# A two-block model's last stage: expert weights in 2 MB pieces and nine slots, one expert gathered ahead, output summed and normed as rows

## The reference

```python
h2 = modulate(rmsnorm(x, norm2_g[l]), sh2, sc2)
x = x + g2 * ec_moe(h2, router_w[l], exp_w1[l], exp_w3[l], exp_w2[l])
return rmsnorm(x, final_g)

def ec_moe(h, router_w, w1, w3, w2):
    aff = jax.nn.softmax(jnp.einsum('bnd,de->bne', h, router_w), axis=-1)
    gates, idx = lax.top_k(jnp.swapaxes(aff, 1, 2), cap)
    xg = jax.vmap(lambda hb, ib: hb[ib])(h, idx)
    a = jnp.einsum('becd,edf->becf', xg, w1)
    b = jnp.einsum('becd,edf->becf', xg, w3)
    y = jnp.einsum('becf,efd->becd', jax.nn.silu(a) * b, w2)
    y = y * gates[..., None]
    return scatter_add(y, idx)
```

## Time and profile before

| | |
|---|---|
| Median of 3 runs | 2808.36 us (2807.79 to 2813.71) |
| The profiled execution | 2808.7 us |
| its span, first to last instruction | 2806.9 us |
| TensorE busy | 2324.2 us, 83% |
| VectorE, ScalarE busy | 776.9 and 345.4 us |
| DMA | 709.05 MB (here of a million bytes), mean 253 GB/s |
| mean granted TensorE clock | 0.883 of 2.4 GHz |

### The profile page before, as it was taken

One profiled execution on the slowest core, in us unless ns is written; L12 is line 12 of the kernel. 1 busy time (PEld: TensorE's weight loads), 2 busy tenths in 40 slices (PEclk: granted clock), 3 DMA queues, 4 the chain that ended last, 5 costly groups with the idle time before them and its releaser, 6 DMA issues.

```text
span 2806.9 us, 34475 instructions
## 1 busy us (share of the span) xinstructions
PE 2324.2 (83%) x14480; PEld 1578.5 (56%) x14480; DVE 776.9 (28%) x1449; ACT 345.4 (12%) x600; POOL 8.7 (0%) x13
## 2 busy tenths in 40 slices
PE   6999879999999899899999986896666666666665
PEld 5887668888888689888877766751011111111111
DVE  5555434474001464411043229340000000000001
ACT  1102221101011222111012110210000000000001
POOL 0000000000000100000000000000000000000000
PEclk9999989999999899999999998887777777677677
DMA  8888234886344230144333120479999999999996
GB/s 339 361 343 357 90 135 190 361 343 237 141 164 164 105 135 4 48 159 156 136 120 120 60 75 1 162 308 418 418 416 416 418 418 418 418 417 416 418 418 279
DMA packets 114085, 709.05 MB, mean 253 GB/s; under 512 B 10833, under 2 KB 10961, under 8 KB 44497
## 3 DMA queue, kind: packets, MB, share of 16 engines
q1 hardware_dynamic: 114000, 707.80, 63.1%
HBM read 706.71 MB, written 1.05 MB: 252 GB/s over the span
## 4 chain that ended last, share of the span: by engine, by line
PE 62%; DMA 25%; DVE 7%; SPq 4%; ACT 1%; issue 1%; DVEq 0%; ACTq 0%
DMA ring<-in_w 17%; PE ps L656 11%; PE ps L670 11%; PE ps L663 11%; DMA sq<-in_w 6%; PE ps L699 5%; PE ps L1009 4%; PE ps L815 4%; SPq L558 3%; PE ps L1189 2%; PE ps L629 1%; PE ps L1227 1%; PE ps L1007 1%; PE ps L1216 1%; PE ps L728 1%
## 5 line engine op out<-in xcount | busy, mean ns | idle before, releaser
L656 PE MATMUL ps<-hT,arena 128*128 128x256 f32 x1408 | 325.6, 385 | 10.0 <-ACT hT L1303 10.0
L663 PE MATMUL ps<-hT,arena 128*128 128x256 f32 x1408 | 318.2, 379 | 0.0
L670 PE MATMUL ps<-hid,arena 128*128 128x256 f32 x1408 | 311.1, 379 | 0.0
L656 PEld LDWEIGHTS ps<-hT,arena 128*128 128x128 f32 x1408 | 271.9, 194 | 53.2 <-issue 15.2
L663 PEld LDWEIGHTS ps<-hT,arena 128*128 128x128 f32 x1408 | 267.5, 190 | 36.4
L670 PEld LDWEIGHTS ps<-hid,arena 128*128 128x128 f32 x1408 | 267.5, 190 | 36.4
L1189 PE MATMUL ps<-ring,arena 128*32 128x512 f32 x1024 | 172.4, 770 | 79.7 <-DMA ring<-in_w 78.1
L1275 ACT ACTIVATE arena<-ps 128x512 f32<-128x512 f32 (+5 forms) x152 | 95.9, 641 | 1014.6 <-PE ps L1206 316.2
L1189 PE MATMUL ps<-arena 128*32 128x512 f32 x768 | 146.6, 855 | 81.7 <-DMA arena<-in_w 81.7
L1216 PE MATMUL ps<-arena 128*32 128x512 f32 x768 | 132.2, 793 | 78.1 <-DMA arena<-in_w 65.9
L1664 DVE TENSOR_TENSOR hid<-sil,ps 128x256 f32<-128x256 f32 x88 | 37.1, 421 | 577.1 <-ACT sil L1313 576.8
(11 more groups left out here) (347 smaller groups left out, 2117.8 us busy)
## 6 DMA issues: line engine op xcount, KB each, us to landing
arena<-in_w SPq DMA_DIRECT2D x192, 1024.0 KB, 24.0
ring<-in_w SPq DMA_DIRECT2D x128, 1024.0 KB, 20.7
arena<-in_ada SPq DMA_DIRECT2D x96, 1024.0 KB, 10.4
ring<-in_ring_w SPq DMA_DIRECT2D x52, 1024.0 KB, 4.9
arena<-in_ffn_gate SPq DMA_DIRECT2D x44, 1024.0 KB, 5.7
arena<-in_ffn_up SPq DMA_DIRECT2D x44, 1024.0 KB, 6.4
arena<-in_ffn_down SPq DMA_DIRECT2D x44, 1024.0 KB, 4.8
hT<-in_w SPq DMA_DIRECT2D x32, 1024.0 KB, 18.1
```

The costliest lines, as they stand in the source:

```text
L656: last = mm(ps[:, ft, 0:T], gate3[:, kt, ft * P:(ft + 1) * P], h3[:, kt, :], start=kt == 0, stop=kt == KT - 1)
L663: last = mm(ps[:, ft, T:2 * T], up3[:, kt, ft * P:(ft + 1) * P], h3[:, kt, :], start=kt == 0, stop=kt == KT - 1)
L670: last = mm(acc(m), down3[:, ft, m * P:(m + 1) * P], hid3[:, ft, :], start=False, stop=True, skip_group_check=True)
```

## The change

- The host lays the weights out anew, as one array `experts` of pieces of 2 MB, 12 for each expert: four of w1, four of w3, four of w2, each with one contiguous row of 16 KB for each partition.
- There are nine slots of 2 MB: six places of `arena`, two halves of `ring`, and `hT` and `sq` together (now one tensor `hT_sq`). SyncE issues two loads and `earlier` after `hy_mixed`, four loads after `hg_out`, two as the projection frees the ring, one after the third `e_turned`, and each later one when the piece nine back is used.
- The logits come first, with the router as the weights (eight matmuls of 256 columns) and are then transposed; the transposes of `h` follow them. Spreading needs 16 rooms in other banks. VectorE ranks expert 0 alone, then experts 1 to 15.
- `picked(e)` makes one expert's tokens and its way back: 16 matmuls of 32 columns, two transposes. It is called for expert e + 1 between the second and the third piece of w2 of expert e. The big gather and `way_back` are gone.
- The output is summed as rows (tokens on the partitions) in four banks; `x` is put there by 16 matmuls during expert 0, the gate is applied to `e_y` by VectorE, and the last norm works along the rows: a square with a sum, a root and a reciprocal of one column, two products and a store of half the output for each 128 tokens.
- The experts are straight code on all engines in place of hardware loops.

The core of the diff (blank lines taken out):

```diff
+    w13 = np.stack([np.asarray(i["exp_w1_2"])[0], np.asarray(i["exp_w3_2"])[0]], 1)
+    w13 = w13.reshape(NE, 8, 2, P, EFF).transpose(0, 1, 3, 2, 4).reshape(NE, 8, P, 2 * EFF)
+    w2 = np.asarray(i["exp_w2_2"])[0].reshape(NE, 4, 4, P, D).transpose(0, 1, 3, 2, 4).reshape(NE, 4, P, 4 * D)
+    out["experts"] = np.concatenate([w13, w2], 1).reshape(NE * PER_EXPERT, P, 2 * SLOT)
...
+        hT_sq = sb("hT_sq", 2 * KT * T)
+        hT, sq = hT_sq[:, 0:KT * T], hT_sq[:, KT * T:]
...
+        e_slots = [ar(n, 2 * SLOT) for n in (0, 2 * SLOT, 13056, 19200, 19200 + 2 * SLOT, 19200 + 4 * SLOT)] \
+            + [ring[:, 0:2 * SLOT], ring[:, 2 * SLOT:], hT_sq[:, :]]
+        E_RING = len(e_slots)
...
+            def expert_load(n):
+                if n >= E_RING:
+                    sp.wait_ge(sem("moe_slot"), n - E_RING + 1)
+                sp.dma_start(e_slots[n % E_RING], a["experts"][n, :, :]).then_inc(sem(E_LANDED[n % E_RING][0]), 16)
...
+            sp.wait_ge(sem("hy_mixed"), 4)
             sp.dma_start(e_early.rearrange("p a b -> p (a b)"), a["earlier"]).then_inc(sem("early_landed"), 16)
...
-            with sp.Fori(0, NE - 1) as e:
-                for j in range(E_RING, PER_EXPERT):
-                    sp.wait_ge(sem("moe_slot"), PER_EXPERT * e + (j - E_RING + 1))
-                    expert_load(e, j)
...
+            for n in range(2):
+                expert_load(n)
+            sp.wait_ge(sem("hg_out"), 1)
+            for n in range(2, 6):
+                expert_load(n)
+            for n in range(6, 8):
+                sp.wait_ge(sem("proj_slot"), 8 + 2 * (n - 6) + 2)
+                expert_load(n)
+            sp.wait_ge(sem("e_turned"), 3)
+            for n in range(8, PER_EXPERT * NE):
+                expert_load(n)
+            for tt in range(TT):
+                sp.wait_ge(sem("row_ready"), tt + 1)
+                sp.dma_start(out[tt * P:(tt + 1) * P, :], o_row[:, tt, :]).then_inc(sem("out_stored"), 16)
...
+            def routing():
+                for kt in range(KT):
+                    h_part(9, kt)
+                    last = mm(ps[0:NE, 4, 0:T], v("rw", kt * NE, NE), h3[:, kt, :], start=kt == 0, stop=kt == KT - 1)
+                last.then_inc(sem("e_turned"), 1)
+                pe.wait_ge(sem("e_rows"), 1)
...
                 for tt in range(TT):
                     for kt in range(KT):
-                        last = mm(ps[:, 4, tt * NE:(tt + 1) * NE], h3[:, kt, tt * P:(tt + 1) * P], v("rw", kt * NE, NE),
-                                  start=kt == 0, stop=kt == KT - 1)
+                        last = tr(ps[:, 2 * tt + kt // 4, (kt % 4) * P:(kt % 4 + 1) * P], h3[:, kt, tt * P:(tt + 1) * P], ident)
                 last.then_inc(sem("e_turned"), 1)
...
+                pe.wait_ge(sem("e_rows"), 4)
+                spread(range(0, 12))
+            def spread(es):
+                for e in es:
+                    if e >= 12:
+                        pe.wait_ge(sem("e_ranked"), (e | 1) - 11)
+                    mm(spread_room(e), ident[0:NE, e:e + 1].to_broadcast([NE, P]), e_row[0:NE, :], start=True, stop=True) \
+                        .then_inc(sem("e_spread"), 1)
+            def picked(e):
+                pe.wait_ge(sem("moe_pick"), e + 1)
+                x_out, back_out = picked_room(e)
+                for kt in range(KT):
+                    for tt in range(TT):
+                        last = mm(x_out[:, kt * CAP:(kt + 1) * CAP], e_h[:, tt, kt * P:(kt + 1) * P], e_pick[:, tt, :],
+                                  start=tt == 0, stop=tt == 1)
+                for tt in range(TT):
+                    last = tr(back_out[:, tt * P:(tt + 1) * P], e_wide[:, tt, :, :].rearrange("p r c -> p (r c)"), ident)
+                last.then_inc(sem("moe_back"), 1)
...
+                picked(0)
+                spread(range(12, NE))
                 for e in range(NE):
...
+                            if kt % 2 == 0:
+                                w = weights(n0 + 4 * part + kt // 2)
                             for n in range(4):
-                                last = mm(ps[32 * n:32 * n + 32, part, :], e_xe[:, kt, :], w[:, n * 512:(n + 1) * 512],
+                                last = mm(ps[32 * n:32 * n + 32, part, :], e_xe[:, kt, :],
+                                          w[:, (kt % 2) * SLOT + n * 512:(kt % 2) * SLOT + (n + 1) * 512],
                                           start=kt == 0, stop=kt == KT - 1, skip_group_check=True)
-                            last.then_inc(sem("moe_slot"), 1)
-                    if first:
-                        pe.wait_ge(sem("e_select"), 3)
...
-                        way_back()
...
+                            if kt % 2 == 1:
+                                last.then_inc(sem("moe_slot"), 1)
...
+                    if e == 0:
...
+                        for tt in range(TT):
+                            for kt in range(KT):
+                                mm(rows(tt)[:, kt // 4, (kt % 4) * P:(kt % 4 + 1) * P], x3[:, kt, tt * P:(tt + 1) * P], ident,
+                                   start=kt % 4 == 0, stop=True, skip_group_check=True)
...
+                    for n in range(4):
+                        if n == 2 and e < NE - 1:
+                            picked(e + 1)
+                        w = weights(n0 + 8 + n)
+                        for i in range(4):
...
+                    for tt in range(TT):
                         for nn in range(2):
                             r = slice(64 * nn, 64 * nn + 64)
-                            last = mm(half(4, 4 * nn + i), e_y[r, i * P:(i + 1) * P], e_bk[r, :],
+                            last = mm(rows(tt)[:, nn, :], e_bk[r, tt * P:(tt + 1) * P], e_y[r, :],
                                       start=False, stop=True, skip_group_check=True)
...
-                with pe.Fori(1, NE) as e:
-                    expert(e)
...
+                act.wait_ge(sem("e_turned"), 3)
+                copy(e_h, ps[:, 0:4, :].rearrange("p (t b) c -> p t (b c)", t=TT)).then_inc(sem("e_rows"), 1)
...
+            def picked(e):
+                x_out, back_out = picked_room(e)
+                act.wait_ge(sem("moe_back"), e + 1)
+                copy(e_xe, tiles(x_out, CAP)).then_inc(sem("moe_x"), 1)
+                if e > 0:
+                    act.wait_ge(sem("moe_o"), e)
+                copy(e_bk, back_out).then_inc(sem("moe_bk"), 1)
...
+                    if e < NE - 1:
+                        picked(e + 1)
+                for tt in range(TT):
+                    act.wait_ge(sem("rows_ready"), tt + 1)
+                    f(sq[:, tt * D:(tt + 1) * D].rearrange("p (b c) -> p b c", b=2), rows(tt), ACT.Square, scale=D ** -0.5,
+                      accum_out=e_st[:, 10 + tt:11 + tt]).then_inc(sem("row_sums"), 1)
+                for tt in range(TT):
+                    act.wait_ge(sem("row_vars"), tt + 1)
+                    f(e_st[:, 12 + tt:13 + tt], e_st[:, 12 + tt:13 + tt], ACT.Sqrt).then_inc(sem("row_roots"), 1)
...
+                select(0, 1)
+                pick(0)
+                select(1, NE)
+            def pick(e):
+                cp(e_pick, e_sel[:, :, e, :])
...
+                    last = ts(e_wide[:, tt], bcm(e_sel[:, tt, e, :], P // CAP), e_aff[:, tt, e:e + 1], None, ALU.mult)
+                last.then_inc(sem("moe_pick"), 1)
...
+                    if e < NE - 1:
+                        dve.wait_ge(sem("moe_back"), e + 1)
+                        pick(e + 1)
...
+                    dve.wait_ge(sem("moe_slot"), PER_EXPERT * (e + 1))
+                    tt_(e_y, ps[:, 3, :], e_gate, ALU.mult).then_inc(sem("moe_y"), 1)
...
+                for tt in range(TT):
+                    dve.wait_ge(sem("row_sums"), tt + 1)
+                    ts(e_st[:, 12 + tt:13 + tt], e_st[:, 10 + tt:11 + tt], EPS, None, ALU.add).then_inc(sem("row_vars"), 1)
+                for tt in range(TT):
+                    dve.wait_ge(sem("row_roots"), tt + 1)
+                    done(nc.vector.reciprocal(e_st[:, 12 + tt:13 + tt], e_st[:, 12 + tt:13 + tt]))
+                    for nn, g in enumerate((sil, hid)):
+                        last = stt(out=o_row[:, tt, nn * 512:(nn + 1) * 512], in0=rows(tt)[:, nn, :],
+                                   scalar=e_st[:, 12 + tt:13 + tt], in1=g[:, :], op0=ALU.mult, op1=ALU.mult)
+                    last.then_inc(sem("row_ready"), 1)
```

286 lines of the change are left out of this document (88 added, 198 removed).

## The result

The changed kernel takes **2764.86 us** (median of 4 runs, 2761.80 to 2767.13), the kernel before, beside it, 2809.33 us (2807.79 to 2813.71). The ratio is 0.9837, with an interval of 0.9826 to 0.9849: 44 us or 1.6% less, clear of the interval. The forecast was 2764 us.

The account below looks back on a forecast made before the run. The experts' weight stream over saturated DMA engines was taken as the bound, with its start and tail. Terms -15.1, -5, -20.9, +5.6 and -9.4 sum to -44.8 from a 2806.9 us span, giving 2764 us, range 2750 to 2785.

Parts of the forecast that it names:

- term 1: Loads ahead of the first expert: 18 MB in instead of 12, so 6 pieces fewer to come, -15.1 us.
- Term 2: Routing ahead of expert 0: first slot free at 1839.3 instead of 1844.4, -5 us (ends 0 and -10).
- Term 3: Experts' weight stream: 16 KB rows lower a MB's price from 2.512 to 2.455 us, -20.9 us.
- Term 4: TensorE's straight expert code: about 28 more code pages over the same DMA engines, 0.2 us each, +5.6 us.
- 5. TensorE's added work: Experts' stage: picked(e+1) between w2 pieces, 39 us an expert becomes 45 of 58.9, hidden by the stream, 0.
- Term 6: Tail after the last landing: 14.5 us instead of 23.8, -9.4 us (ends -6 and -12).
- A: Rival, experts' stream: the rate doesn't follow the row length; 2776 us, or 2785 with no gain; chance 0.13.
- B: Rival, code fetch: pages share one DMA engine, +28 us instead of +5.6, so 2786 us; chance 0.08.
- E: Rival, weight reads: a power-of-two row pitch slows them; loses past 2.62 us a piece, 2854 us at 2.70; chance 0.01.
- C: Rival, experts' stage: TensorE becomes the bound, slower than before; 2835 us at 64 us an expert; chance 0.03.
- D: Rival, start and end: early loads are not early or the row tail is as long; 2778 us; chance 0.07.
- the mark set for term 2: Sign at the stream's start: a first slot freed after 1845 would make the prediction wrong at term 2.

Follow-up runs that it names:

- split gather: Against the changed kernel: six spreads instead of twelve ahead of the first gather, two behind it, eight behind expert 0's first two pieces; 2757.93 us.
- the loop: Against the changed kernel: TensorE's code for experts 4 to 12 is a loop of three rounds over three experts, others written out; 2759.98 us.

## Why the prediction was right

The time was right to 1 us, with errors that cancelled.

| Term | Forecast | Measured | From |
|---|---|---|---|
| 1. 18 MB ahead | -15.1 | -15.1 | 6 MB at the price of before; nine loads were out, and three pieces held back cost 14.9 |
| 2. first slot freed | -5 | +0.9 | 1845.31 against 1844.39 |
| 3. rate | -20.9 | -23.8 | 366 x (2.512 - 2.447) |
| 4. code pages | +5.6 | +5.8 | 852.28 - 173 x 4.893 |
| 5. TensorE's added work | 0 | 0 | DMA share 1.01, TensorE 532 of 800 us |
| 6. tail | -9.4 | -11.5 | 12.35 us for 23.8 |
| Sum | -44.8 | -43.7 | span: -44.0 |

**Term 2 is the step that failed.** Its order of events came true, and the start of spreading within a microsecond (1820.54, forecast 1821), its durations did not, for it let the clock rise halfway: 9.7 us for twelve spreads (10.38), 4.6 for picked(0) (7.04 + 0.67), 1.8 for four spreads (3.78), 2.2 for the first 2 MB (3.3, from 1842.01 to the load at 1845.31). All four at half clock is the end "0" that the text gave; it came out 0.9 us beyond it. The text took its prices from the earlier trace rows, where the old gather ran in 5.67 us because the low clock ended within it. This window of the kernel before, in the columns of the windows above, shows the rise:

```profile
1836.00:1837.00 1.00, 1.00 (x8) 1.00 (x7) 1.00 (x7) 0.28 (x2) 0.00 (x0) 0.62 0.00 0
```

In the new order the clock fell within the first spreads and stayed at 0.50 to between 1844.5 and 1845, so almost nothing of this path got the faster price. The split gather gives back what the term promised: 5.0 to 7.6 us between the first spread and the first slot.

**Term 3 had the right cause and a short size.** Going from 4 to 8 KB rows was worth 0.060 us a MB, and the text took half of that for the next doubling, then a little more by the earlier trace rows. It was 2.489 - 2.447 = 0.042, better than the far end of 2.45. The runs with shorter rows return the old prices: landing slopes of 5.006 and 5.144 us a piece against 4.926, or 14.5 and 39.8 us over 366 MB. How the -18.0 us of terms 3 and 4 together divide depends on the even spacing that is taken: with 4.90 for 4.893 us term 3 is -22.7 and term 4 +4.6.

**Term 4 was right as a sum, its parts less so.** A page costs 0.14 us by the loop, so 27 pages in the stream (one before) explain 3.8 of the 5.8 us. The other 2 us (0.8 us by the spacing of 4.90) are open; they are there with the loop as well. In a sentence by itself: by the Trainium skill (Runtime: NRT & Kernel Launch, "Instruction fetch mechanics") straight code's crossings are mostly hidden. For TensorE's own waits nothing here speaks against it, but by the price above the term isn't 0 in a stream that is full. A page of 16 KB at 427 GB/s would be 0.04 us, so its bytes alone don't make the 0.14.

**Term 6** took 3 us for the last weights and 2 to 3.8 for the out product; at the full clock they took 1.92 and 1.99. At the low one this end takes up to 15.75 us: the forecast of 14.5 lay between the two.

**The rivals.** A fell by the runs with shorter rows, B by the sum of term 4, E by the pitch (its break-even counts the 15.1 us of term 1 twice: with 15.1 less it is 2.58 us a MB, not 2.62). C fell too: between 1895 and 2752 us TensorE waits for a landing in front of 132 of the 174 pieces, at a granted clock of 0.80, even higher than before (0.73). That is most of them, as the text asked. D came half true: the start gave nothing, the end all and more. Of the signs that the text named, the slices (426 forecast, 427) and the last store within 12 us of the last landing (both halves issued by 2760.20, 9.7 us after it) came, and so did the period (12 x 4.926 = 59.1 us) and the pages (94 against 68, 26 more). The first waiting transfer at 1839 did not come, and at 1845.31 stands just beyond the mark set for term 2. The last landing near 2743 did not come either: it was at 2750.55. The text's own sum puts it at 2762.1 - 14.5 = 2747.6, so 2743 was a slip; of the 2.95 us by which even the sum missed, the shorter end took 2.15 back.

## What to carry to other kernels

In a stage that only streams, the time is the moment of the first freed slot plus bytes times a price, so read the chain ahead of that moment as closely as the stage itself: work that the first consumer doesn't need belongs behind it, and a microsecond gained ahead of the first slot is a microsecond at the end. Lay streamed weights with long contiguous rows for each partition (16 KB was the best and the longest tried), and let every transfer span all 128 partitions. Judge edits of 1 to 2 us by the slope between distant landings, not by medians that a start and an end scatter.

## What was not expected of the hardware

Transfers into 64 partitions moved 214 GB/s with the DMA engines' share at 1.01, against 427 with 128: the busy share alone doesn't tell a slow stream from a fast one.

TensorE's low clock came in stretches that the records show as busy, and not in the same place in every execution. From the first spread to the first waiting load it took 24.8 us in four profiles (changed kernel, rows of 4 KB, both kernels with 8 KB rows) and 22.2 in four others with the same instructions there (loads of 64 partitions, 20 KB pitch, 6 MB held back, loop); the clock fell within 1 us of the first spread in the first four, more than 3 us behind it in the others. The end took 12.3 to 15.8 us. Each kernel has only one profile, so it isn't shown, but these two and the start of the spreads (1818.08 to 1823.02) are large enough to explain the 2 to 9 us between runs of one kernel.
